# Moving 32x32 blocks by way of DRAM on one queue, an unrolled loop, and a later take-up of the moved blocks

## The chip, the cores and the metric

One core of one Trainium2 chip. The metric is the device time of one execution in microseconds; the kernel before has a median of 2729.89 us in 3 runs (2728.75 to 2730.19).

## The reference

Two transformer blocks in a row on 256 tokens of width 2048, all in float32. Each block normalises its input, makes projections, mixes tokens (block one with two kinds of softmax attention, block two with a chunked recurrence and a gated attention), adds the result, runs a feed-forward network, and ends with a gated embedding. The change touches the two feed-forward networks and what leads in and out of them:

```
ff = jnp.square(jax.nn.relu(u2 @ w_up)) @ w_down                     # block one, width 8192
a, g = jnp.split(u @ w_up, 2, axis=-1)                               # block two, width 5632
a = causal_dwconv(a, conv_w, conv_b)
x = x + (jax.nn.gelu(a, approximate=False) * g) @ w_down
```

## The kernel before, in words

**Products.** Each float32 weight is split on the chip into a high and a low part, and each activation too, so that a product is three passes of TensorE: high by high, high by low, low by high. A *unit* is 512 output columns for 256 tokens over 16 tiles of 128 rows: 16 x 2 x 3 = 96 matmuls (L2259 to L2261). A unit is cut into eight *halves* of two tiles, 12 matmuls each.

**Weights.** SyncE's queue loads them (L402) in pieces of 1 MB, two halves each, into a ring of four (`raw`). For each half ScalarE makes the high part (`hi`, L642) and VectorE the low part (`lo`, L1344), into a ring of four slots (`split`). Both engines run three halves ahead of TensorE (`LEAD`): in step m of a unit they prepare half m+3, when TensorE has given a slot back, and then do what `after(m)` asks for. In `after(m)` TensorE is therefore in half m.

**Why blocks are moved.** A unit comes out with tokens on the partitions. The next product wants features there. VectorE transposes 32x32 blocks in place within 32 partitions (L1742, L1744 for the feed-forward units, L1395 for rows of the residual), into `cross`; what is left is to carry each 32-partition group to its place. `move_blocks` (L377) does this with 16 DMAs of 32 KB from SBUF to SBUF: eight on SyncE's queue (between two weight loads, by `wide_and_move`) and eight on GpSimd's. Each queue first waits for `blocks_made`. There are 47 such moves: 3 in `branch`, 16 in `ffn1`, 3 in `out2`, 22 in `ffn2` and `ffn2b`, 3 in the last down product.

**Who takes a move up.** ScalarE or VectorE waits for both queues (`wait_for_move`, L385):
- `ffn1` (block one, four turns of 4 up and 4 down units): ScalarE and VectorE make the operand `X2` of the down product (`finish`, L936 and L1752) at m = 4 and m = 12 of the two-unit step that follows; the last of a turn, `finish(3)`, is taken up at m = 4 of the first down step, and half 6 of that unit is the first to read it.
- `ffn2` (block two, eleven pairs of up units a and g): for a, ScalarE copies the moved block at m = 12 (L1258), VectorE runs the convolution at m = 13 (L2116 to L2122) and ScalarE the gelu at m = 14; for g, VectorE multiplies at m = 3 of the next step (`gate_hidden`, L2104), and `finish` follows at m = 4.
- `out2` and the last down product: ScalarE takes the moved rows up (`gained_hi_moved`, L702) four halves after the unit's end.

**Loops.** TensorE, ScalarE and VectorE run turn 0 of `ffn1` written out, turns 1 and 2 as a loop of two (L1025, L1852, L2534), and turn 3 written out again. SyncE runs all four as a loop.

GpSimd has little else: rows of gains, and `ple_kept`, a DRAM scratch that it writes (L601) and later reads back (L620); `gate_rows` is another (L605 to L611).

Of the kernel before, what the change touches and what calls it, by code (L numbers as in the profile page):

```python
# [176 lines left out]
def two_blocks(nc, a, out):  # L177
# [141 lines left out]
    moved_by_sp, moved_by_pool = sem("moved_by_sp"), sem("moved_by_pool")  # L319
    second_by_sp, second_by_pool = sem("second_by_sp"), sem("second_by_pool")  # L320
# [22 lines left out]
    OUT2 = DOWN = plan([wide2, wide2])  # L343
    DOWN3 = [(m // 4 % 2, "wide", X2, 2 * (m % 4), 2, m % 4 == 0, False) for m in range(8)]
# [25 lines left out]

    MIX_MOVES, FFN1_MOVES, OUT2_MOVES, FFN2_MOVES, DOWN3_MOVES = 0, 3, 19, 22, 44
    MIX_MOVED = [E[:, 4 * c:4 * c + 4, :].rearrange("p k t -> p (k t)") for c in range(3)]
    DOWN3_ROUTES = [(cross_flat, t_flat), (a_moved, g_moved), (cross_flat, t_flat)]
    DOWN3_BY_SP = [moved_by_sp, second_by_sp, moved_by_sp]
    DOWN3_BY_POOL = [moved_by_pool, second_by_pool, moved_by_pool]

    def move_blocks(queue, n, dst, quadrants, moved, src=cross_flat):  # L377

        queue.wait_ge(blocks_made, n + 1)
        for a in quadrants:  # L380
            for b in range(4):
                rows = src[32 * a:32 * a + 32].rearrange("p (q b c) -> p q b c", q=2, b=4)[:, :, b, :]
                queue.dma_start(dst[32 * b:32 * b + 32].rearrange("p (q a c) -> p q a c", q=2, a=4)[:, :, a, :], rows).then_inc(moved, 16)  # L383

    def wait_for_move(eng, n):  # L385

        eng.wait_ge(moved_by_sp, 128 * (n + 1))
        eng.wait_ge(moved_by_pool, 128 * (n + 1))
# [5 lines left out]
    def _(sp):  # L394
# [54 lines left out]
        for n in range(4):  # L449
            s = at_triple("branch", n, 3 * n)  # L450
            wide(s, 0, w_in, 8192 + n * WIDE)
            wide(s, 4, a["w_br_moba"][0], n * WIDE, rows=512)
            if n:
                move_blocks(sp, MIX_MOVES + n - 1, MIX_MOVED[n - 1], (0, 1), moved_by_sp)
            wide(s, 5, a["w_br_moba"][0], n * WIDE, 512, 512)
            wide(s, 6, a["w_br_diff"][0], n * WIDE, rows=1024)
# [15 lines left out]
        def wide_and_move(at, w, col0, row0, n, dst):  # L472

            wide(at, 0, w, col0, row0, 512)
            if n is not None:
                move_blocks(sp, n, dst, (0, 1), moved_by_sp)
            wide(at, 1, w, col0, row0 + 512, 1536)

        def ffn1(b):
            for u in range(8):  # L480
                s = At("ffn1", g=4 * u, u=u, outer_turn=b * 8, outer_units=b * 8)
                n = FFN1_MOVES + b * 4 + (u - 2) if 2 <= u < 6 else None
                if u < 4:
                    wide_and_move(s, a["w_up"][0], b * 2048 + u * WIDE, 0, n, t_flat)
                else:
                    wide_and_move(s, a["w_down"][0], (u - 4) * WIDE, b * 2048, n, t_flat)
# [22 lines left out]
        for u in range(4):  # L509
            wide_and_move(At("out2", g=4 * u, u=u), a["w_out_2"][0], u * WIDE, 0, OUT2_MOVES + u - 2 if u > 1 else None, t_flat)  # L510

        def ffn2(name, b, pairs, c0):

            outer = dict(outer_turn=b * 12, outer_units=b * 12)
            col0 = c0 * WIDE

            def dst(u):
                return g_moved if u % 2 else a_moved

            for u in range(2 * pairs):  # L520
                n = FFN2_MOVES + 2 * c0 + u - 2 if u > 1 else OUT2_MOVES + 2 if c0 + u == 0 else None
                wide_and_move(At(name, g=4 * u, u=u, **outer), a["w_up_2"][0], u % 2 * FF2 + col0 + u // 2 * WIDE, 0, n, t_flat if c0 + u == 0 else dst(u))
            last = FFN2_MOVES + 2 * c0 + 2 * pairs - 2
            w = a["w_down_2"][0]
            if name == "ffn2":
                for n in range(4):
                    wide_and_move(At(name, g=8 * pairs + 4 * n, u=2 * pairs + n, **outer), w, n * WIDE, col0, last + n if n < 2 else None, dst(n))
            else:
                s = At(name, g=8 * pairs, u=2 * pairs)
                wide(s, 0, w, 0, col0, 512)  # L530
                move_blocks(sp, last, dst(0), (0, 1), moved_by_sp)
# [3 lines left out]
                move_blocks(sp, last + 1, dst(1), (0, 1), moved_by_sp)  # L535
# [3 lines left out]
                for n in range(2):  # L539
                    src, moved_to = DOWN3_ROUTES[n]  # L540
                    move_blocks(sp, DOWN3_MOVES + n, moved_to, (0, 1), DOWN3_BY_SP[n], src)
                    wide(s, 10 + n, w, 3 * WIDE, col0 + 512 + 512 * n, 512)
# [5 lines left out]
        move_blocks(sp, DOWN3_MOVES + 2, t_flat, (0, 1), moved_by_sp)  # L548
# [15 lines left out]
    def _(pool):  # L564
# [13 lines left out]
        for n in range(3):  # L578
            move_blocks(pool, MIX_MOVES + n, MIX_MOVED[n], (2, 3), moved_by_pool)
# [11 lines left out]
        for n in range(16):  # L591
            move_blocks(pool, FFN1_MOVES + n, t_flat, (2, 3), moved_by_pool)
# [21 lines left out]
        for n in range(3):  # L614
            move_blocks(pool, OUT2_MOVES + n, t_flat, (2, 3), moved_by_pool)
        for n in range(FFT2 // 2):
            move_blocks(pool, FFN2_MOVES + n, g_moved if n % 2 else a_moved, (2, 3), moved_by_pool)
# [3 lines left out]
        for n in range(3):  # L621
            src, moved_to = DOWN3_ROUTES[n]
            move_blocks(pool, DOWN3_MOVES + n, moved_to, (2, 3), DOWN3_BY_POOL[n], src)


    @block.scalar
    def _(act):
# [310 lines left out]
        def ffn1(b):  # L938
# [86 lines left out]
        loop(act, steps, 3, 0, ffn1, start=1)  # L1025
# [207 lines left out]
        def ffn2(name, b, pairs, c0):  # L1233
# [6 lines left out]
            def up(i):  # L1240
# [3 lines left out]
                def after(m):  # L1244
# [7 lines left out]
                    if m == 4 and i:  # L1252
                        finish(i - 1)
# [12 lines left out]
            def down(i):  # L1266
                each_half(At(name, i, 8, 2, g=8 * pairs, u=2 * pairs, **outer), DOWN, lambda m: finish(pairs - 1) if i == 0 and m == 4 else None)

            def last_down(s):

                def after(m):
                    if m == 4:
                        finish(pairs - 1)
                    if m in (14, 16, 22):
# [3 lines left out]
                        if n == 1:  # L1278
                            act.wait_ge(second_by_sp, 128)
                            act.wait_ge(second_by_pool, 128)  # L1280
                        else:
                            wait_for_move(act, DOWN3_MOVES + n // 2)
# [49 lines left out]
    def _(dve):  # L1332
# [421 lines left out]
        def ffn1(b):  # L1754
# [7 lines left out]
            def up(i):  # L1762
                s = At("ffn1", i, 8, 2, **outer)

                def after(m):
# [6 lines left out]
                    if m == 4 and i:  # L1772
                        finish(2 * i - 1)
                    if m == 12:
# [77 lines left out]
        loop(dve, steps, 3, 0, ffn1, start=1)  # L1852
# [244 lines left out]
        def ffn2(name, b, pairs, c0):  # L2097
# [27 lines left out]
            def up(i):  # L2125
# [3 lines left out]
                def after(m):  # L2129
# [6 lines left out]
                    if m == 3 and i:  # L2136
                        gate_hidden(i - 1)
                    if m == 4 and i:
# [7 lines left out]
            def finish_last(m):  # L2146
                if m == 3:
                    gate_hidden(pairs - 1)
                if m == 4:
                    finish(pairs - 1)  # L2150

            def down(i):
                s = At(name, i, 8, 2, g=8 * pairs, u=2 * pairs, **outer)

                def after(m):
                    if i == 0:
                        finish_last(m)
                    if m % 8 == 7:
                        add_h(s, m, m // 8, 2 * i + m // 8)
                each_half(s, DOWN, after)  # L2160
# [66 lines left out]
    def _(pe):  # L2227
# [306 lines left out]
        loop(pe, Chain(None), 3, 0, ffn1, start=1)  # L2534
# [148 lines left out]
        def ffn2(name, b, pairs, c0):  # L2683
# [12 lines left out]
            if name == "ffn2":  # L2696
                for i in range(2):
                    each_half(At(name, i, 8, 2, g=8 * pairs, u=2 * pairs, **outer), DOWN, hidden)
# [36 lines left out]
```

## Time and profile before

| what | value |
|---|---|
| median of 3 runs | 2729.89 us |
| the profiled execution | 2728.78 us, its span 2726.8 us |
| TensorE busy | 2715.3 us of the span, at the full granted clock throughout |
| VectorE, ScalarE, GpSimd busy | 1640.6, 1395.3, 220.0 us |
| DMA engines busy | 5 to 6 tenths in most slices |
| moved by DMA | 546.93 MB |

How to read it: an engine's busy time counts its own instructions, not its waiting for semaphores; DMA issues count on GpSimd and not on SyncE. The time of an idle stretch stands in front of the instruction that ended it, with what released it; "issue" means that the profile shows nothing that the engine waited for.

### The profile page before, as it was taken

How to read it: one execution, taken by the hardware profiler on the slowest of the kernel's cores; microseconds unless marked ns; L12 is line 12 of the kernel's file. 1: busy time of each engine (PE TensorE's matmuls, PEld its weight loads, DVE VectorE, ACT ScalarE, POOL GpSimd, SP SyncE). 2: the span in 40 equal slices, each digit the busy share in tenths (PEclk: the TensorE clock that was granted, in tenths of full speed). 3: DMA queues.
4: the chain of work that ended last, by engine and by line, in shares of the span. 5: the costliest groups of instructions: out<-in, count | busy, mean ns of one | idle time of the engine just before them, and what ended most of it. 6: DMA issues, size and time to landing. Idle time of an engine off the chain costs nothing.

```text
span 2726.8 us, 33571 instructions
## 1 busy us (share of the span) xinstructions
PE 2715.3 (100%) x12786; PEld 2267.8 (83%) x12786; DVE 1640.6 (60%) x2002; ACT 1395.3 (51%) x1851; POOL 220.0 (8%) x410
## 2 busy tenths in 40 slices
PE   9999999999999999999999999999999999999999
PEld 7888888888888878888888888888888888888887
DVE  7666665556555555555566656665666566656665
ACT  6454554446544535445466555655545345435553
POOL 0000000100100101101000000001111011101210
PEclk9999999999999999999999999999999999999999
DMA  8555556665666656656656655556666566656674
GB/s 300 174 181 185 170 176 207 204 203 182 211 213 200 219 191 201 215 179 220 221 176 221 193 162 180 169 170 215 200 218 224 190 203 207 233 189 220 219 244 139
DMA packets 344770, 546.93 MB, mean 201 GB/s; under 512 B 20548, under 2 KB 135184, under 8 KB 343984
## 3 DMA queue, kind: packets, MB, share of 16 engines
q1 hardware_dynamic: 330016, 522.98, 57.9%
q0 software_dynamic: 14608, 21.93, 3.1%
q8 instruction: 100, 1.64, 0.2%
q14 instruction: 46, 0.38, 0.0%
HBM read 515.98 MB, written 4.21 MB: 191 GB/s over the span
## 4 chain that ended last, share of the span: by engine, by line
PE 96%; DVE 2%; ACT 1%; issue 0%; DMA 0%; POOL 0%; SPq 0%; ACTq 0%; DVEq 0%
PE ps L2259 26%; PE ps L2260 25%; PE ps L2261 25%; PE ps L2249 11%; PE ps L2251 6%; DVE split L1344 1%; PE pw L2397 0%; PE pw L2364 0%; PE pw L2322 0%; PE pw L2375 0%; PE pw L2370 0%; ACT split L642 0%; DMA G<-cross 0%; PE pw L2363 0%; PE pw L2613 0%
## 5 line engine op out<-in xcount | busy, mean ns | idle before, releaser
L1344 DVE TENSOR_TENSOR split<-raw,split 128x1024 fp32r<-128x1024 f32 x960 | 1167.3, 1222 | 901.6 <-ACT split L642 899.9
L642 ACT ACTIVATE split<-raw 128x1024 fp32r<-128x1024 f32 x960 | 1009.9, 1058 | 1018.6 <-PE ps L2261 903.4
L2259 PE MATMUL ps<-split,X 128*128 128x512 f32 x3128 | 1221.8, 391 | 2.0 <-DVE split L1344 1.1
L2260 PE MATMUL ps<-split,X 128*128 128x512 f32 x3128 | 1217.2, 389 | 1.7 <-issue 1.7
L2261 PE MATMUL ps<-split,X 128*128 128x512 f32 x3128 | 1217.4, 389 | 0.0
L2259 PEld LDWEIGHTS ps<-split,X 128*128 128x128 f32 x3128 | 587.1, 188 | 125.6 <-issue 3.0
L2260 PEld LDWEIGHTS ps<-split,X 128*128 128x128 f32 x3128 | 587.2, 188 | 122.8 <-issue 2.1
L2261 PEld LDWEIGHTS ps<-split,X 128*128 128x128 f32 x3128 | 587.1, 188 | 122.3
L2249 PE MATMUL ps<-X,split 128*128 128x512 f32 x896 | 282.8, 397 | 0.2 <-DVE split L1344 0.2
L2251 PEld LDWEIGHTS ps<-X,split 128*128 128x128 f32 x896 | 168.3, 188 | 39.7
L2251 PE MATMUL ps<-X,split 128*128 128x256 f32 x896 | 176.1, 278 | 0.0
L383 POOL DMA_DIRECT2D t<-cross x168 | 89.8, 542 | 962.2 <-DVE cross L1744 562.5
L2249 PE MATMUL ps<-split,X 128*128 128x512 f32 x512 | 162.8, 399 | 0.0
L383 POOL DMA_DIRECT2D G<-cross x176 | 93.9, 542 | 583.7 <-DVE cross L1744 561.3
L2249 PEld LDWEIGHTS ps<-X,split 128*128 128x128 f32 x896 | 137.0, 189 | 1.7 <-issue 1.0
L2251 PEld LDWEIGHTS ps<-split,X 128*128 128x128 f32 x512 | 96.2, 188 | 22.7
L2251 PE MATMUL ps<-split,X 128*128 128x256 f32 x512 | 100.7, 278 | 0.0
L2249 PEld LDWEIGHTS ps<-split,X 128*128 128x128 f32 x512 | 78.2, 189 | 0.6 <-issue 0.4
L927 ACT ACTIVATE t<-ps,norm_col 128x512 f32<-128x512 f32 x76 | 47.9, 681 | 43.0 <-PE ps L2261 43.0
L648 ACT ACTIVATE cross<-ps 128x512 f32<-128x512 f32 x44 | 26.3, 597 | 66.5 <-PE ps L2251 66.3
L1742 DVE STREAM_TRANSPOSE cross<-t 128x512 f32<-128x512 f32 x38 | 27.0, 709 | 48.7 <-ACT t L975 37.9
L1262 ACT ACTIVATE G<-G,cols 128x256 f32<-128x256 f32 x44 | 18.8, 498 | 32.1 <-DVE G L2122 32.1
(271 smaller groups left out, 1083.3 us busy)
## 6 DMA issues: line engine op xcount, KB each, us to landing
raw<-in_w_up SPq DMA_DIRECT2D x152, 1024.0 KB, 5.3
raw<-in_w_in SPq DMA_DIRECT2D x134, 1024.0 KB, 5.1
raw<-in_w_down SPq DMA_DIRECT2D x108, 1024.0 KB, 5.2
raw<-in_w_out SPq DMA_DIRECT2D x32, 1024.0 KB, 5.1
raw<-in_w_ple_gate SPq DMA_DIRECT2D x32, 1024.0 KB, 5.2
raw<-in_w_br_moba SPq DMA_DIRECT2D x8, 1024.0 KB, 5.2
raw<-in_w_br_diff SPq DMA_DIRECT2D x8, 1024.0 KB, 6.8
G<-cross SPq DMA_DIRECT2D x176, 32.0 KB, 1.9
```

What stands on the lines that cost most here:

```text
L383: queue.dma_start(dst[32 * b:32 * b + 32].rearrange("p (q a c) -> p q a c", q=2, a=4)[:, :, a, :], rows).then_inc(moved, 16)
L642: A(split[:, k % RING, :, 0, :], raw[:, (k // 2) % RING, HALF * (k % 2):HALF * (k % 2) + HALF, :], ACT.Copy).then_inc(hi_done, 1)
L648: A(cross[:, s], ps[:, 2 * s:2 * s + 2, TOK:512], ACT.Copy).then_inc(cross_done, 1)
L927: ins = A(t_tok[:, q, :], ps[:, bank + q, :], func, scale=norm_col[:, k, q:q + 1])
L1262: ins = A(gelu[:, j, :], conv[:, j, :], ACT.Gelu, bias=vec("conv_b_2", 4 * c + j))
L1344: TT(split[:, k % RING, :, 1, :], raw[:, (k // 2) % RING, HALF * (k % 2):HALF * (k % 2) + HALF, :], split[:, k % RING, :, 0, :], ALU.subtr ...
L1742: nc.vector.transpose(cross_tok[:, 0, :], by_blocks(t_tok[:, 0, :]))
L2249: MM(ps[:, 2 * s + j, :], stay[:, 0, j * P:j * P + P], move, start=start, stop=False, skip_group_check=True)
L2251: ins = MM(ps[:, 2 * s + j, 0:TOK], stay[:, 1, j * P:j * P + P], move[:, 0, :], start=False, stop=stop, skip_group_check=True)
L2259: MM(dst, x_hi, w[:, :, 0, :], start=start, stop=False, skip_group_check=True)
L2260: MM(dst, x_hi, w[:, :, 1, :], start=False, stop=False, skip_group_check=True)
L2261: ins = MM(dst, x_lo, w[:, :, 0, :], start=False, stop=stop, skip_group_check=True)
```

## The change: what it does

- A move is four writes of 128 KB from `cross` to a DRAM scratch (two scratches in turn, `blocks_kept`), a wait on GpSimd until all four have landed, and one read of 512 KB back to the destination. All five are on GpSimd's queue; SyncE's queue carries no moves any more.
- The three loops over turns 1 and 2 of `ffn1` are written out.
- Take-up is later: in `ffn1` m = 4 and 12 of the up steps become 5 and 13; in `ffn2` m = 3 and 4 become 5 and 6. ScalarE's copy of a at m = 12, `finish(3)` at m = 4 of the first down step of `ffn1`, and the take-up in `out2` and in the last down product at m = 14, 16, 22 stay.
- The first two down units of each `ffn2` are interleaved (`DOWN2`): 12 tiles of unit 0, 12 tiles of unit 1, then the last 4 of each, and SyncE loads the weights in that order. The last 4 tiles are those of the last pair.

```diff
-    def move_blocks(queue, n, dst, quadrants, moved, src=cross_flat):
-
-        queue.wait_ge(blocks_made, n + 1)
-        for a in quadrants:
-            for b in range(4):
-                rows = src[32 * a:32 * a + 32].rearrange("p (q b c) -> p q b c", q=2, b=4)[:, :, b, :]
-                queue.dma_start(dst[32 * b:32 * b + 32].rearrange("p (q a c) -> p q a c", q=2, a=4)[:, :, a, :], rows).then_inc(moved, 16)
+    def move_blocks(pool, n, dst, src=cross_flat):
+
+        pool.wait_ge(blocks_made, n + 1)
+        kept = blocks_kept[n % 2]
+        for a in range(4):
+            rows = src[32 * a:32 * a + 32].rearrange("p (q b c) -> p q b c", q=2, b=4)
+            pool.dma_start(kept.rearrange("(b i) (q a c) -> i q b a c", b=4, q=2, a=4)[:, :, :, a, :], rows).then_inc(blocks_left[n % 2], 16)
+        pool.wait_ge(blocks_left[n % 2], 64 * (n // 2 + 1))
+        pool.dma_start(dst, kept).then_inc(blocks_back[n % 2], 16)
 
     def wait_for_move(eng, n):
 
-        eng.wait_ge(moved_by_sp, 128 * (n + 1))
-        eng.wait_ge(moved_by_pool, 128 * (n + 1))
+        eng.wait_ge(blocks_back[n % 2], 16 * (n // 2 + 1))
...
+    DOWN2 = [(m // 6, "wide", X2, 2 * (m % 6), 2, m % 6 == 0, False) for m in range(12)]
+    DOWN2 += [(m // 2, "wide", X2, 12 + 2 * (m % 2), 2, False, m % 2 == 1) for m in range(4)]
...
-                    wide_and_move(s, a["w_up"][0], b * 2048 + u * WIDE, 0, n, t_flat)
+                    wide(s, 0, a["w_up"][0], b * 2048 + u * WIDE)
...
-                    if m == 4 and i:
+                    if m == 5 and i:
                         finish(2 * i - 1)
-                    if m == 12:
+                    if m == 13:
                         finish(2 * i)
...
-                    if m == 3 and i:
+                    if m == 5 and i:
                         gate_hidden(i - 1)
-                    if m == 4 and i:
+                    if m == 6 and i:
                         finish(i - 1)
...
-                each_half(s, DOWN, after)
+                    if m in ((7, 15) if i else (13, 15)):
+                        add_h(s, m, m // 15, 2 * i + m // 15)
+                each_half(s, DOWN if i else DOWN2, after)
...
-        loop(pe, Chain(None), 3, 0, ffn1, start=1)
+        ffn1(1)
+        ffn1(2)
         ffn1(3)
```

The same three lines stand for ScalarE and VectorE.

## Rows read from the trace of the kernel before

**Rows 1.** The page: the span, and busy us, share and instructions by engine.

```profile
span 2726.8 us, 33571 instructions
PE 2715.3 (100%) x12786; PEld 2267.8 (83%) x12786; DVE 1640.6 (60%) x2002; ACT 1395.3 (51%) x1851; POOL 220.0 (8%) x410
```

**Rows 2.** Stretches of 68 us: busy us and instructions by engine, clock, DMA.

```profile
884.00:952.00 68.00, 68.00 (x301) 56.31 (x301) 37.89 (x37) 36.26 (x44) 12.80 (x24) 1.00 0.66 218
...
1020.00:1088.00 68.00, 66.29 (x292) 54.54 (x291) 34.57 (x33) 32.20 (x38) 8.53 (x16) 1.00 0.62 203
...
2312.00:2380.00 68.00, 67.31 (x297) 55.45 (x297) 42.56 (x49) 33.00 (x38) 12.81 (x24) 1.00 0.67 224
...
2652.00:2720.00 68.00, 68.00 (x302) 56.31 (x301) 37.05 (x38) 29.38 (x31) 0.00 (x0) 1.00 0.45 152
```

**Rows 3.** Timeline of TensorE, 1017 to 1025 us: start, duration, what.

```profile
1019.24 0.49 PE L2259 MATMUL ps<-split,X 128*128 128x512 f32 x1 [0.16 <-issue]
...
1022.83 0.50 PE L2260 MATMUL ps<-split,X 128*128 128x512 f32 x1 [1.71 <-issue]
```

**Rows 4.** Timelines around 2310 to 2327 us, by engine, in order of time.

```profile
2310.21 0.67 DVE L1744 STREAM_TRANSPOSE cross<-t 128x512 f32<-128x512 f32 x1
...
2314.27 4.28 POOL L383 DMA_DIRECT2D G<-cross  x8 [22.17 <-issue]
...
2316.03 10.94 SPq L402 DMA_DIRECT2D raw<-in_w_up  x3
...
2324.21 1.23 DVE L2104 TENSOR_TENSOR G<-G 128x1024 f32<-128x1024 f32 x1 [6.65 <-DMA G<-cross]
...
2326.71 0.47 PE L2259 MATMUL ps<-split,X 128*128 128x512 f32 x1 [0.69 <-DVE split L1344]
```

**Rows 5.** GpSimd's DMA issues by line: count, busy us, mean ns of one.

```profile
L601 POOL DMA_DIRECT2D ple_kept<-E x4 | 2.9, 721 | 41.6 <-ACT E L906 41.6
L583 POOL DMA_DIRECT2D sg<-in_w_in x3 | 3.5, 1166 | 37.9 <-DVE G L1670 37.9
```

**Rows 6.** Timeline of GpSimd, 1511 to 1530 us: a write to DRAM, its read.

```profile
1512.86 0.53 POOL L607 DMA_DIRECT2D gate_rows<-E  x1 [3.96 <-DVE E L1933]
1515.40 0.57 POOL L609 DMA_DIRECT2D G<-gate_rows  x1 [2.01 <-DMA gate_rows<-E]
```

**Rows 7.** DMA issues: KB each, median us from issue to landing.

```profile
G<-cross POOLq DMA_DIRECT2D x176, 32.0 KB, 1.8
...
ple_kept<-E POOLq DMA_DIRECT2D x4, 512.0 KB, 4.3
...
E<-ple_kept POOLq DMA_DIRECT2D x2, 1024.0 KB, 10.3
...
G<-gate_rows POOLq DMA_DIRECT2D x1, 512.0 KB, 5.8
```

**Rows 8.** Timelines of VectorE and ScalarE, 758 to 784 us (`ffn1`, `finish(3)`).

```profile
760.65 0.67 DVE L1744 STREAM_TRANSPOSE cross<-t 128x512 f32<-128x512 f32 x1
...
768.94 1.06 ACT L642 ACTIVATE split<-raw 128x1024 fp32r<-128x1024 f32 x1 [1.66 <-PE ps L2261]
769.90 1.14 ACT L936 ACTIVATE X<-t 128x512 fp32r<-128x512 f32 x2
...
771.17 1.29 DVE L1752 TENSOR_TENSOR X<-t,X 128x512 fp32r<-128x512 f32 x2
```

**Rows 9.** Timelines of three engines, 2240 to 2284 us (`ffn2`, a unit a).

```profile
2243.10 0.67 DVE L1744 STREAM_TRANSPOSE cross<-t 128x512 f32<-128x512 f32 x1
...
2244.06 4.26 POOL L383 DMA_DIRECT2D G<-cross  x8 [15.67 <-DVE cross L1744]
...
2253.65 1.04 ACT L1258 ACTIVATE E<-G 128x1024 f32<-128x1024 f32 x1
2255.40 1.06 ACT L642 ACTIVATE split<-raw 128x1024 fp32r<-128x1024 f32 x1 [0.71 <-PE ps L2261]
...
2262.10 1.22 DVE L1344 TENSOR_TENSOR split<-raw,split 128x1024 fp32r<-128x1024 f32 x1
```

More of the change, by code:

```diff
@@ L318, in two_blocks @@
     tokens_kept, blocks_made, padded = (sem(n) for n in ("tokens_kept", "blocks_made", "padded"))
-    moved_by_sp, moved_by_pool = sem("moved_by_sp"), sem("moved_by_pool")
-    second_by_sp, second_by_pool = sem("second_by_sp"), sem("second_by_pool")
+    blocks_left, blocks_back = ([sem(f"{name}{k}") for k in range(2)] for name in ("blocks_left", "blocks_back"))
     out_landed = sem("out_landed")
@@ L369, in squared @@
         return 8 * (k - 1)
+    blocks_kept = [nc.dram_tensor(f"blocks_kept{k}", (P, 1024), F32).ap() for k in range(2)]
     MIX_MOVES, FFN1_MOVES, OUT2_MOVES, FFN2_MOVES, DOWN3_MOVES = 0, 3, 19, 22, 44
@@ L451, in _ @@
             wide(s, 0, w_in, 8192 + n * WIDE)
[L452 to L455, printed above, removed]
+            wide(s, 4, a["w_br_moba"][0], n * WIDE, rows=1024)
             wide(s, 6, a["w_br_diff"][0], n * WIDE, rows=1024)
@@ L470, in _ @@
         proj("proj1", a["w_ple_proj"][0])
[L472 to L477, printed above, removed]
         def ffn1(b):
@@ L481, in ffn1 @@
                 s = At("ffn1", g=4 * u, u=u, outer_turn=b * 8, outer_units=b * 8)
-                n = FFN1_MOVES + b * 4 + (u - 2) if 2 <= u < 6 else None
                 if u < 4:
-                    wide_and_move(s, a["w_up"][0], b * 2048 + u * WIDE, 0, n, t_flat)
+                    wide(s, 0, a["w_up"][0], b * 2048 + u * WIDE)
                 else:
-                    wide_and_move(s, a["w_down"][0], (u - 4) * WIDE, b * 2048, n, t_flat)
+                    wide(s, 0, a["w_down"][0], (u - 4) * WIDE, b * 2048)
         loop(sp, Chain(None), 4, 0, ffn1)
@@ L509, in _ @@
         for u in range(4):
-            wide_and_move(At("out2", g=4 * u, u=u), a["w_out_2"][0], u * WIDE, 0, OUT2_MOVES + u - 2 if u > 1 else None, t_flat)
+            wide(At("out2", g=4 * u, u=u), 0, a["w_out_2"][0], u * WIDE)
         def ffn2(name, b, pairs, c0):
@@ L515, in ffn2 @@
             col0 = c0 * WIDE
-            def dst(u):
-                return g_moved if u % 2 else a_moved
             for u in range(2 * pairs):
-                n = FFN2_MOVES + 2 * c0 + u - 2 if u > 1 else OUT2_MOVES + 2 if c0 + u == 0 else None
-                wide_and_move(At(name, g=4 * u, u=u, **outer), a["w_up_2"][0], u % 2 * FF2 + col0 + u // 2 * WIDE, 0, n, t_flat if c0 + u == 0 else dst(u))
-            last = FFN2_MOVES + 2 * c0 + 2 * pairs - 2
+                wide(At(name, g=4 * u, u=u, **outer), 0, a["w_up_2"][0], u % 2 * FF2 + col0 + u // 2 * WIDE)
             w = a["w_down_2"][0]
             if name == "ffn2":
-                for n in range(4):
-                    wide_and_move(At(name, g=8 * pairs + 4 * n, u=2 * pairs + n, **outer), w, n * WIDE, col0, last + n if n < 2 else None, dst(n))
+                s = At(name, g=8 * pairs, u=2 * pairs, **outer)
+                wide(s, 0, w, 0, col0, 512)
+                wide(s, 1, w, 0, col0 + 512, 1024)
+                wide(s, 3, w, WIDE, col0, 1024)
+                wide(s, 5, w, WIDE, col0 + 1024, 512)
+                wide(s, 6, w, 0, col0 + 1536, 512)
+                wide(s, 7, w, WIDE, col0 + 1536, 512)
+                for n in range(2, 4):
+                    wide(s, 4 * n, w, n * WIDE, col0)
             else:
@@ L530, in ffn2 @@
                 wide(s, 0, w, 0, col0, 512)
-                move_blocks(sp, last, dst(0), (0, 1), moved_by_sp)
                 wide(s, 1, w, 0, col0 + 512, 512)
@@ L534, in ffn2 @@
                 wide(s, 4, w, 0, col0 + 1024, 512)
-                move_blocks(sp, last + 1, dst(1), (0, 1), moved_by_sp)
                 wide(s, 5, w, WIDE, col0 + 1024, 512)
@@ L538, in ffn2 @@
                 wide(s, 9, w, 3 * WIDE, col0, 512)
[L539 to L542, printed above, removed]
+                wide(s, 10, w, 3 * WIDE, col0 + 512, 1024)
         ffn2("ffn2", 0, 4, 0)
@@ L547, in _ @@
         wide(At("gate2"), 0, w, 0, 0, 1024)
-        move_blocks(sp, DOWN3_MOVES + 2, t_flat, (0, 1), moved_by_sp)
         wide(At("gate2"), 2, w, 0, 1024, 1024)
@@ L578, in _ @@
         for n in range(3):
-            move_blocks(pool, MIX_MOVES + n, MIX_MOVED[n], (2, 3), moved_by_pool)
+            move_blocks(pool, MIX_MOVES + n, MIX_MOVED[n])
         pool.wait_ge(gated, 4)
@@ L591, in _ @@
         for n in range(16):
-            move_blocks(pool, FFN1_MOVES + n, t_flat, (2, 3), moved_by_pool)
+            move_blocks(pool, FFN1_MOVES + n, t_flat)
         pool.wait_ge(hid_ready, 32)
@@ L614, in _ @@
         for n in range(3):
-            move_blocks(pool, OUT2_MOVES + n, t_flat, (2, 3), moved_by_pool)
+            move_blocks(pool, OUT2_MOVES + n, t_flat)
         for n in range(FFT2 // 2):
-            move_blocks(pool, FFN2_MOVES + n, g_moved if n % 2 else a_moved, (2, 3), moved_by_pool)
+            move_blocks(pool, FFN2_MOVES + n, g_moved if n % 2 else a_moved)
         pool.wait_ge(hid_ready, 32 + FFT2 // 2)
@@ L622, in _ @@
             src, moved_to = DOWN3_ROUTES[n]
-            move_blocks(pool, DOWN3_MOVES + n, moved_to, (2, 3), DOWN3_BY_POOL[n], src)
+            move_blocks(pool, DOWN3_MOVES + n, moved_to, src)
     @block.scalar
@@ L1024, in _ @@
         A(gate_split[:, :, 16:32], gate_w[:, :, :], ACT.Copy, scale=0.0).then_inc(gate_split_hi, 1)
-        loop(act, steps, 3, 0, ffn1, start=1)
+        ffn1(1)
+        ffn1(2)
         ffn1(3)
@@ L1266, in down @@
             def down(i):
-                each_half(At(name, i, 8, 2, g=8 * pairs, u=2 * pairs, **outer), DOWN, lambda m: finish(pairs - 1) if i == 0 and m == 4 else None)
+                each_half(At(name, i, 8, 2, g=8 * pairs, u=2 * pairs, **outer), DOWN if i else DOWN2, lambda m: finish(pairs - 1) if i == 0 and m == 6 else None)
             def last_down(s):
                 def after(m):
-                    if m == 4:
+                    if m == 6:
                         finish(pairs - 1)
@@ L1277, in after @@
                         square_h(8, n)
[L1278 to L1282, printed above, removed]
+                        wait_for_move(act, DOWN3_MOVES + n)
                         gained_hi_moved(n, "ple_norm_g_2", DOWN3_ROUTES[n][1])
@@ L1771, in after @@
                             norm_inverse(2)
-                    if m == 4 and i:
+                    if m == 5 and i:
                         finish(2 * i - 1)
-                    if m == 12:
+                    if m == 13:
                         finish(2 * i)
@@ L1851, in _ @@
         TT(gate_split[:, :, GATE_LO:GATE_LO + 16], gate_w[:, :, :], gate_split[:, :, 0:16], ALU.subtract).then_inc(gate_split_lo, 1)
-        loop(dve, steps, 3, 0, ffn1, start=1)
+        ffn1(1)
+        ffn1(2)
         ffn1(3)
@@ L2135, in after @@
                             norm_inverse(7)
-                    if m == 3 and i:
+                    if m == 5 and i:
                         gate_hidden(i - 1)
-                    if m == 4 and i:
+                    if m == 6 and i:
                         finish(i - 1)
@@ L2146, in finish_last @@
             def finish_last(m):
-                if m == 3:
+                if m == 5:
                     gate_hidden(pairs - 1)
-                if m == 4:
+                if m == 6:
                     finish(pairs - 1)
@@ L2157, in after @@
                         finish_last(m)
-                    if m % 8 == 7:
-                        add_h(s, m, m // 8, 2 * i + m // 8)
-                each_half(s, DOWN, after)
+                    if m in ((7, 15) if i else (13, 15)):
+                        add_h(s, m, m // 15, 2 * i + m // 15)
+                each_half(s, DOWN if i else DOWN2, after)
             def last_down(s):
@@ L2533, in _ @@
         ffn1(0)
-        loop(pe, Chain(None), 3, 0, ffn1, start=1)
+        ffn1(1)
+        ffn1(2)
         ffn1(3)
@@ L2697, in ffn2 @@
                 for i in range(2):
-                    each_half(At(name, i, 8, 2, g=8 * pairs, u=2 * pairs, **outer), DOWN, hidden)
+                    each_half(At(name, i, 8, 2, g=8 * pairs, u=2 * pairs, **outer), DOWN if i else DOWN2, hidden)
             else:
```

2 lines of the change are left out of this document (removed).

## The prediction

> **What bounds the kernel now.** I read the page first: TensorE is busy for 2715.3 of 2726.8 us [rows 1], so time can be won only where TensorE stands still, or lost where something new makes it stand still. Next the stretches of 68 us. A stretch of the feed-forward networks that holds 24 of GpSimd's move DMAs has 301 matmuls, and one at the end with none has 302 [rows 2]: a matmul every 68/301 = 0.226 us, a half of 12 matmuls every 2.71 us, with moves or without. In the stretches that the change touches, two fall clearly short: 292 from 1020 us and 297 from 2312 us [rows 2]. That is 9 + 4 = 13 missing matmuls, 13 x 0.226 = 2.9 us. What stood there is in the timelines. At 1019 and 1022 us TensorE is idle for 0.16 and 1.71 us and waits for nothing the profile knows [rows 3]; this is where the loop over turns 1 and 2 of `ffn1` jumps back. At 2326 us it waits 0.69 us for a low part [rows 4]: VectorE stood 6.65 us before L2104, because one move, ready when the transposes ended at 2310.88, came late: GpSimd began its DMAs only at 2314.27 (3.4 us late, the cause not in the profile), and its last ones ran into three weight loads issued from 2316.03 [rows 4]. So at most 2.9 us, 0.11%, can be won here.
>
> **What each part costs or gives.**
>
> Loops written out: the same matmuls in the same order, without a jump. Gives the idle at 1019 and 1022 us, 9 x 0.226 = 2.0 us. ScalarE's and VectorE's loops cost nothing before, since both run ahead of TensorE.
>
> Later take-up: the late move at 2310.88 landed 2324.2 - 2310.88 = 13.3 us after its transposes and cost 4 x 0.226 = 0.9 us [rows 2, 4], so L2104 at m = 3 bears a landing up to 13.3 - 0.9 = 12.4 us; at m = 5 it bears two halves more, 12.4 + 5.4 = 17.8 us. That returns the 0.9 us if a hiccup like it comes again. The last pair would then be finished at m = 6 of a down unit whose half 6 reads it; `DOWN2` reads it from step 12 instead, 6 x 2.71 = 16 us after the take-up, so this costs nothing. Interleaving keeps every matmul; the third unit starts at step 16, and the first one's sums are read from step 13, 5.4 us earlier in TensorE's time than they are needed. If VectorE were late there by more, TensorE would wait at step 16.
>
> SyncE's queue: 47 x 8 DMAs and 47 waits leave it. Nothing waits for it (no weight load shows among TensorE's releasers in [rows 3, 4]), so this gives nothing by itself. But the eight DMAs held weight loads back during a move; now loads run beside every move, as at 2316 us.
>
> GpSimd's queue: 16 short DMAs on two queues become four writes, a wait and a read on one. Behind the new wait stand the next move, the gain rows and the read-back of `ple_kept`; moves come one per unit, 96 x 0.226 = 21.7 us apart, except in the last down product, where the second follows two halves after the first and would start behind its read. Three moves there and three in `out2` keep their take-up four halves after the unit's end; each is a single event of a us or so and is left to the range. For the time from the transposes' end to landing, no row shows the very thing, so step by step:
> - start: 2244.06 - 2243.77 = 0.3 us [rows 9];
> - three issues before the last write: 0.54 each for 64 pieces (4.26/8) [rows 9], 1.17 for 2048 pieces [rows 5]; I take 0.72, `ple_kept` with as many pieces as here, 256 [rows 5]: 2.2 us;
> - last write issued to read issued: the small write to `gate_rows` took 1515.40 - 1512.86 = 2.5 us [rows 6]; the 512 KB write to `ple_kept` 4.3 to land [rows 7], plus 0.3 to start again, 4.6. At 128 KB I take the middle, 3.5;
> - the read, 512 KB: between 1.8 (32 KB from SBUF) and 10.3 (1 MB of `ple_kept`); I take 5.8, the read of 512 KB of `gate_rows`, the same size on the same queue [rows 7].
>
> Sum 0.3 + 2.2 + 3.5 + 5.8 = 11.8 us; ends 0.3 + 1.6 + 2.5 + 1.8 = 6.2 and 0.3 + 3.5 + 4.6 + 10.3 = 18.7. The Trainium skill ("DMA: Bandwidth & Descriptors", Anatomy of one DMA) gives 2.0 us and bytes/436e3 per DMA from GpSimd and warns that most of the 2 us is the write receipt, longest for HBM. By its figures the estimate would be about 0.3 + 2.2 + 2.6 + 3.2 = 8.3 us, but it would put 3.2 us on a 512 KB write and the row has 4.3, so the rows decide.
>
> What bears 11.8 us? Two take-ups were not made later.
> - `finish(3)`, four times: transposes end at 761.32, half 4 starts about 768.9, so half 6, the first reader, at 768.9 + 5.4 = 774.3. Before it lie one L936 (half of 1.14) and one L1752 (half of 1.29), together 1.2 us [rows 8]. The limit is 774.3 - 1.2 - 761.3 = 11.8 us.
> - ScalarE's copy of a, eleven times: transposes end at 2243.77, the copy starts at 2253.65, 9.9 us later. A later start first uses up 0.71 us of ScalarE's idle before L642 at 2255.40. Then it pushes the convolution and the low part behind it, which ends at 2263.3; the slot that L642 fills at 2255.4 is read three halves later, the next one at 2255.4 + 4 x 2.71 = 2266.2, so 2.9 us are left [rows 9]. The limit is 9.9 + 0.7 + 2.9 = 13.5 us.
>
> At 11.8 us the first limit is just met and the second holds with 1.7 us in hand: cost 0. Each us past 11.8 costs 4 us in all, past 13.5 another 11, past 17.8 (g) another 11.
>
> **Sum.** Against the profiled execution, 2728.78 (span 2726.8 and 2.0 around it): 2728.78 - 2.0 - 0.9 = 2725.9. It lies 1.1 below the median of 2729.89, so 2727.0 on the scale of the medians. About 0.2% (5.5 us) is what a measurement of this kernel can tell from no change; this is half of it.
>
> **Rivals.**
> 1. *The round trip outlasts the slack* (0.13). Place: L936 in `finish(3)` and L1258. For it: loads now run beside every move, and beside loads 32 KB DMAs had the late move end at 13.3 us. Against it: the rows used for 5.8 and 4.3 ran beside weight loads too, and the slack is measured. At 15 us it costs 4 x 3.2 + 11 x 1.5 = 29 us: 2756. It turns the sign past the 0.2% at 2727.0 + 4d = 2735.4, d = 2.1, a landing of about 13.7 us (the eleven add 2 there); at the upper end, 18.7 us, it is 4 x 6.9 + 11 x 5.2 + 11 x 0.9 = 95 us, 2822.
> 2. *The change does not do what it seems to* (0.13). The idle at 1022 us is "issue", so that the jump causes it is my reading; written-out code could stall likewise at another place, and a slow start of GpSimd like that at 2310.88 can fall on a move of a, where 11.8 + 3.1 = 14.9 us passes both limits once. Then 2730.
> 3. *TensorE's pace itself rises* (0.04), because transfers no longer go from SBUF to SBUF. One ns per matmul is 12786 ns: 2714. Against it stand 301 matmuls with moves and 302 without [rows 2].
>
> **How the numbers follow.** My case, landing under 13.3 us and the jump's idle gone, has 0.70: 2727.0, from 2725.0 (the lowest run, 2728.75, less 2.9, and 0.8 for chance) to 2727.0 + 4 x 1.5 = 2733. Rivals 1, 2 and 3 have 0.13, 0.13 and 0.04. The range 2725 to 2733 holds my case and rival 2, 0.83; the two others, 0.17, are left out, and so are the extreme ends of the landing. Faster by over 0.2% is rival 3, slower is rival 1, the rest is the same.
>
> **What would show it.** Right: no idle of TensorE over 1 us after 700 us; 301 matmuls in every stretch inside a feed-forward network; the last of `cross`'s four writes landing about 5.7 us after the transposes and the read 11.8; ScalarE's L1258 waiting for a DMA by up to 2 us and TensorE for nothing. Wrong: TensorE waiting for a low part once per pair of up units at regular distance, or for L1752 at half 6 of each turn's first down unit; an "issue" gap inside turns 1 or 2 of `ffn1`; a read that lands within 8 us, which would make the step-by-step cost too high though not the time; a changed pace in a stretch without gaps.

## The result and the profile after

The changed kernel takes 2805.91 us (median of 6 runs, 2802.20 to 2811.39) against 2729.92 us before: a ratio of 1.0281 [1.0271, 1.0291], slower by 76 us. The forecast was 2727.0, a small gain, with a range of 2725 to 2733; the change came out as a loss, far outside the range. What happened is rival 1, the round trip outlasting the slack, at a higher price than the rival had been given. The profiled execution took 2802.2 us, with a span of 2800.4.

The page of the changed kernel, its span and engines, the chain that ended last, and DMA issues with the median from issue to landing:

```profile
span 2800.4 us, 32690 instructions
...
PE 2738.1 (98%) x12786; PEld 2275.8 (81%) x12786; DVE 1635.5 (58%) x2002; ACT 1390.0 (50%) x1851; POOL 160.2 (6%) x269
...
PE 78%; DMA 10%; DVE 7%; ACT 2%; issue 2%; POOL 2%; ACTq 0%; POOLq 0%; DVEq 0%
...
blocks_kept<-cross POOLq DMA_DIRECT2D x184, 128.0 KB, 5.8
G<-blocks_kept POOLq DMA_DIRECT2D x23, 512.0 KB, 6.2
t<-blocks_kept POOLq DMA_DIRECT2D x21, 512.0 KB, 4.5
```

Beside [rows 1], TensorE stands still for 2800.4 - 2738.1 = 62.3 us instead of 11.5, and needs 22.8 us more for the same 12786 matmuls. DMA now has 10% of the chain that ended last. A write of 128 KB takes 5.8 us, and the estimate for the whole way from the last write's issue to the read's issue had been 3.5.

The loss by stage, from the stretches of the changed kernel (columns as in [rows 2]; the first one answers to the stretch with the jump, the next four are `ffn1`, `out2`, `ffn2` with its down units, and the last down product):

```profile
1020.00:1088.00 68.00, 68.00 (x301) 56.31 (x301) 36.70 (x34) 32.93 (x39) 5.99 (x10) 1.00 0.67 217
...
700.00:1420.00 720.00, 715.07 (x3164) 590.41 (x3163) 392.76 (x380) 345.01 (x414) 48.25 (x81) 1.00 0.66 216
...
1885.00:1935.00 50.00, 43.22 (x186) 34.84 (x185) 23.66 (x31) 23.92 (x41) 3.55 (x6) 0.97 0.55 188
...
1935.00:2670.00 735.00, 702.92 (x3031) 573.37 (x3030) 417.35 (x478) 328.39 (x380) 70.92 (x119) 0.98 0.64 216
...
2670.00:2715.00 45.00, 34.64 (x140) 27.82 (x139) 22.37 (x28) 20.96 (x36) 5.13 (x9) 0.89 0.55 184
```

The stretch from 1020 us has its 301 matmuls, where [rows 2] had 292: the jump's idle is gone. For the others, the length less 68/301 = 0.226 us per matmul is what the stretch lost: 720 - 3164 x 0.2259 = 5.2 us in `ffn1`, 8.0 in `out2`, 50.3 in `ffn2`, 13.4 in the last product. Their sum, 76.9, is the whole loss: it equals the difference to the span of the kernel `late_sbuf` below (2723.4), which has everything of the change but the new way of moving (77.0). Of the 50.3 in `ffn2`, 735 - 702.92 = 32.1 are idle; the rest is TensorE running slower, at a mean granted clock of 0.98.

The waits of the changed kernel (us in total, times, longest):

```profile
POOL G L385 <- DMA blocks_kept<-cross: 130.3, 22, 7.0
POOL t L385 <- DMA blocks_kept<-cross: 121.6, 21, 7.1
...
ACT E L1245 <- DMA G<-blocks_kept: 76.9, 11, 9.8
DVE G L2088 <- DMA G<-blocks_kept: 54.6, 11, 6.0
...
ACT X L922 <- DVE G L2088: 52.3, 11, 5.8
...
PE ps L2243 <- DVE split L1327: 43.1, 24, 3.7
...
PE pw L2306 <- DVE h L2060: 6.7, 2, 6.3
PE ps L2243 <- DVE X L1735: 4.4, 4, 1.5
```

TensorE waits 24 times for a low part (43.1 us) and four times for `finish(3)` (4.4), the signs that were named for "wrong", though not once per pair: 17 of the 24 stand in `ffn2` with its eleven pairs. ScalarE's copy of a (L1245, before L1258) waits 7.0 us on average, VectorE's `gate_hidden` (L2088, before L2104) 5.0, although its take-up is two halves later than in [rows 4].

One pair in `ffn2` of the changed kernel, by engine, in order of time: first the move of g, then the move of a.

```profile
1972.79 11.49 SPq L403 DMA_DIRECT2D raw<-in_w_up  x4
...
1976.13 0.67 DVE L1727 STREAM_TRANSPOSE cross<-t 128x512 f32<-128x512 f32 x1
...
1977.09 2.44 POOL L383 DMA_DIRECT2D blocks_kept<-cross  x4 [16.50 <-DVE cross L1727]
1986.16 0.56 POOL L385 DMA_DIRECT2D G<-blocks_kept  x1 [6.64 <-DMA blocks_kept<-cross]
1992.37 1.23 DVE L2088 TENSOR_TENSOR G<-G 128x1024 f32<-128x1024 f32 x1 [5.77 <-DMA G<-blocks_kept]
1993.63 1.16 ACT L922 ACTIVATE X<-G 128x512 fp32r<-128x512 f32 x2 [5.57 <-DVE G L2088]
1995.64 1.24 ACT L913 ACTIVATE t<-ps,norm_col 128x512 f32<-128x512 f32 x2
...
1997.61 0.67 DVE L1727 STREAM_TRANSPOSE cross<-t 128x512 f32<-128x512 f32 x1
...
1998.57 2.44 POOL L383 DMA_DIRECT2D blocks_kept<-cross  x4 [11.85 <-DVE cross L1727]
1999.42 6.64 SPq L403 DMA_DIRECT2D raw<-in_w_up  x3
2003.34 1.06 ACT L628 ACTIVATE split<-raw 128x1024 fp32r<-128x1024 f32 x1 [1.66 <-PE ps L2245]
2007.91 0.56 POOL L385 DMA_DIRECT2D G<-blocks_kept  x1 [6.90 <-DMA blocks_kept<-cross]
2014.16 1.06 ACT L1245 ACTIVATE E<-G 128x1024 f32<-128x1024 f32 x1 [9.76 <-DMA G<-blocks_kept]
2016.19 1.22 DVE L1327 TENSOR_TENSOR split<-raw,split 128x1024 fp32r<-128x1024 f32 x1 [10.54 <-ACT split L628]
2017.34 1.14 DVE L2100 TENSOR_SCALAR G<-E,cols 128x256 f32<-128x256 f32 x4
...
2021.81 1.22 DVE L1327 TENSOR_TENSOR split<-raw,split 128x1024 fp32r<-128x1024 f32 x1
2017.56 0.47 PE L2243 MATMUL ps<-split,X 128*128 128x512 f32 x1 [3.44 <-DVE split L1327]
2019.06 0.63 PE L2243 MATMUL ps<-split,X 128*128 128x512 f32 x1
...
2021.19 0.63 PE L2245 MATMUL ps<-split,X 128*128 128x512 f32 x1
2023.17 0.47 PE L2243 MATMUL ps<-split,X 128*128 128x512 f32 x1 [1.35 <-DVE split L1327]
```

Three readings. **The move is long because loads run beside it.** SyncE issues 1 MB weight loads beside both moves, four from 1972.79 and three from 1999.42; the four writes of a, issued from 1998.57, let GpSimd read back only at 2007.91, and ScalarE's copy starts at 2014.16, 2014.16 - 1998.28 = 15.9 us after the transposes' end. **One late move costs more than one wait.** The copy's delay uses up the lead, so TensorE waits 3.44 us at 2017.56. Then VectorE's convolution (from 2017.34; its three steps take 1.14, 1.67 and 1.67 us) stands between two low parts with no lead left: the next one starts only at 2021.81, and TensorE waits again, 1.35 us at 2023.17. **In between TensorE is slow.** From 2019.06 to 2021.19 a matmul comes every 0.426 us instead of 0.226 (five intervals in 2.13 us). The granted clock of that stretch is 0.50, that is 1.2 GHz, the lower of the clock's two levels; shortly before, the engine had stood still for 3.44 us.

### The profile page after: what moved, and what is told of

The parts are those of the page before. It is cut to its first block, busy times and chain, and to the rows that moved or that the text cites. A ratio compares the mean times of both kernels' runs of the same rounds, so it can differ in the third digit from the quotient of the medians.

```text
span 2800.4 us, 32690 instructions
## 1 busy us (share of the span) xinstructions
PE 2738.1 (98%) x12786; PEld 2275.8 (81%) x12786; DVE 1635.5 (58%) x2002; ACT 1390.0 (50%) x1851; POOL 160.2 (6%) x269
## 4 chain that ended last, share of the span: by engine, by line
PE 78%; DMA 10%; DVE 7%; ACT 2%; issue 2%; POOL 2%; ACTq 0%; POOLq 0%; DVEq 0%
PE ps L2243 19%; PE ps L2245 19%; PE ps L2244 19%; PE ps L2233 11%; PE ps L2235 6%; DMA blocks_kept<-cross 5%; DMA G<-blocks_kept 3%; DVE split L1327 2%; POOL blocks_kept L383 2%; DMA t<-blocks_kept 1%; ACT split L628 1%; DVE G L2103 1%; DVE G L2106 1%; DVE cross L1725 0%; DVE cross L1727 0%
## 5 line engine op out<-in xcount | busy, mean ns | idle before, releaser
L2243 PE MATMUL ps<-split,X 128*128 128x512 f32 x3128 | 1230.9, 394 | 48.1 <-DVE split L1327 43.1
L383 POOL DMA_DIRECT2D blocks_kept<-cross x184 | 112.3, 617 | 1507.5 <-DVE cross L1727 1025.5
L913 ACT ACTIVATE t<-ps,norm_col 128x512 f32<-128x512 f32 x76 | 47.7, 679 | 30.8 <-PE ps L2245 28.0
L1245 ACT ACTIVATE E<-G 128x1024 f32<-128x1024 f32 x11 | 11.7, 1061 | 76.9 <-DMA G<-blocks_kept 76.9
L2088 DVE TENSOR_TENSOR G<-G 128x1024 f32<-128x1024 f32 x11 | 13.5, 1226 | 54.6 <-DMA G<-blocks_kept 54.6
```

The lines of the kernel that those rows point to most:

```text
L383: pool.dma_start(kept.rearrange("(b i) (q a c) -> i q b a c", b=4, q=2, a=4)[:, :, :, a, :], rows).then_inc(blocks_left[n % 2], 16)
L913: ins = A(t_tok[:, q, :], ps[:, bank + q, :], func, scale=norm_col[:, k, q:q + 1])
L2243: MM(dst, x_hi, w[:, :, 0, :], start=start, stop=False, skip_group_check=True)
```

## Experiments

The theory after the result: the new way of moving alone is to blame, because the eight DMAs of SyncE's queue that it removes had kept weight loads away while blocks moved. In the kernel before, SyncE's queue shows this in one pair (timelines of SyncE and, for later, of ScalarE):

```profile
2243.80 5.08 SPq L383 DMA_DIRECT2D G<-cross  x8
2248.92 6.47 SPq L402 DMA_DIRECT2D raw<-in_w_up  x3
...
2252.68 1.06 ACT L642 ACTIVATE split<-raw 128x1024 fp32r<-128x1024 f32 x1 [1.66 <-PE ps L2261]
```

The next load was issued only after the eight transfers, 5.1 us after the move began. Rivals: the written-out loops or the new order of take-up and down units cost the time; or a round trip through DRAM is too slow in itself, loads or not.

**late_sbuf**: the changed kernel's loops, take-up and down order, but the 16 transfers between SBUF partitions on two queues as before. Against the changed kernel, among others:

```diff
+        queue.wait_ge(blocks_made, n + 1)
+        for a in quadrants:
+            for b in range(4):
+                rows = src[32 * a:32 * a + 32].rearrange("p (q b c) -> p q b c", q=2, b=4)[:, :, b, :]
+                queue.dma_start(dst[32 * b:32 * b + 32].rearrange("p (q a c) -> p q a c", q=2, a=4)[:, :, a, :], rows).then_inc(moved, 16)
```

> The written-out loops, the later take-up and DOWN2 of the change, but each move still 16 transfers from SBUF to SBUF on two queues. Theory A (the whole loss comes from the moves through DRAM): 2727 us, 2 to 3 us under the kernel before, no idle of TensorE over 1 us after 700 us. Rival B (interleaving the down units or taking blocks up later costs time by itself): between 2735 and 2805 us, with TensorE waiting in the first down step of each ffn2 or two halves after a unit's end.

Measured: 2725.25 us (11 runs) against 2729.52 for the kernel before (28 runs), ratio 0.9984 [0.9975, 0.9993], span 2723.4. So the whole loss comes from the new way of moving, and the rest of the change gains a little. This run puts back two things at once, the transfers within SBUF and the eight DMAs on SyncE's queue; the runs below tell them apart.

**unrolled**: the kernel before with nothing but the three loops written out.

```diff
-        loop(pe, Chain(None), 3, 0, ffn1, start=1)
+        ffn1(1)
+        ffn1(2)
         ffn1(3)
```

> The kernel before with only the three loops over turns 1 and 2 of ffn1 written out. If the jump makes the idle at 1019 and 1022 us: 2.0 us less than before, 2728 us, and no issue gap inside ffn1. If written-out code stalls elsewhere: 2730 us with an issue gap at another place.

Measured: 2725.99 us (11 runs), ratio 0.9988 [0.9979, 0.9997]: 3.5 us less where 2.0 were expected, by the interval 0.8 to 5.7. Its stretch from 1020 us:

```profile
1020.00:1088.00 68.00, 68.00 (x302) 56.31 (x301) 35.99 (x35) 34.88 (x41) 8.96 (x17) 1.00 0.61 202
```

302 matmuls instead of 292: the jump had caused the "issue" idle. TensorE waits for "issue" nowhere in this run, and the first half of rival 2 falls.

**hold_writes** and **hold_move**: the changed kernel, but SyncE waits at the places where it used to issue its eight DMAs (after the first load of a unit): in one until the four writes have landed, in the other until the read has. No DMA is added. SyncE's loop over the turns of `ffn1` is written out for it.

```diff
+    def hold_loads(sp, n):
+        sp.wait_ge(blocks_left[n % 2], 64 * (n // 2 + 1))     # hold_writes
+        sp.wait_ge(blocks_back[n % 2], 16 * (n // 2 + 1))     # hold_move
```

> The changed kernel, with SyncE's queue waiting, at the places where it issued moves before, until the four writes of the move have landed; only then does it issue further weight loads (and SyncE's loop over ffn1 is written out). Theory C (the writes take 6 us because a weight load is issued beside the third one): the writes land by about 5 us after the transposes instead of 8.2, the read about 11.5 instead of 13.9, time 2730 to 2745 us. Rival I (four writes of 512-byte pieces to DRAM on GpSimd's queue take 8 us whatever runs beside them): writes 8.2, read 12 to 14, time 2790 us or more.

> As hold_writes, but SyncE waits until the read of the move has landed too. Theory C: read back 9 us after the transposes, below every limit, time about 2727 us. Rival I: the move still takes 12 us or more, time over 2780 us; should the held loads themselves come too late, TensorE would wait for ScalarE's high parts released by a DMA of raw.

Measured: hold_writes 2739.27 us (5 runs), ratio 1.0038 [1.0025, 1.0051]; hold_move 2725.40 us (10 runs), ratio 0.9984 [0.9975, 0.9994]. The DMA issues of hold_writes:

```profile
blocks_kept<-cross POOLq DMA_DIRECT2D x184, 128.0 KB, 2.7
G<-blocks_kept POOLq DMA_DIRECT2D x23, 512.0 KB, 6.6
```

and of hold_move:

```profile
blocks_kept<-cross POOLq DMA_DIRECT2D x184, 128.0 KB, 2.7
G<-blocks_kept POOLq DMA_DIRECT2D x23, 512.0 KB, 3.5
```

The same write takes 2.7 us with the loads held and 5.8 beside them (the changed kernel), the same read 3.5 and 6.6 (hold_writes, which lets the loads go when the read starts). In hold_move a whole move reads like this (timelines of GpSimd, SyncE and ScalarE):

```profile
1980.55 2.43 POOL L383 DMA_DIRECT2D blocks_kept<-cross  x4 [14.39 <-DVE cross L1752]
1985.41 0.56 POOL L385 DMA_DIRECT2D G<-blocks_kept  x1 [2.44 <-DMA blocks_kept<-cross]
1988.90 2.98 SPq L407 DMA_DIRECT2D raw<-in_w_up  x3
...
1990.13 1.04 ACT L1270 ACTIVATE E<-G 128x1024 f32<-128x1024 f32 x1
```

The transposes ended at 1980.25 and the loads, released by the landing, start again at 1988.90: 8.65 us for the move. ScalarE's copy comes in its turn and waits for nothing. Holding the loads gives back all 80 us between the changed kernel and this one, with every byte still going through DRAM; so the round trip is not too slow in itself, the loads beside it are the cause. Holding during the writes alone already returns 67 us; the read beside loads keeps 13.9.

**a_later**: the changed kernel with ScalarE's copy of a at m = 14, the convolution at m = 0 of the next step and the gelu at m = 2.

```diff
-                    if m == 12:
+                    if m == 14:
...
-                    if m == 13:
-                        convolve(c)
+                    if m == 0 and i:
+                        convolve(c - 1)
```

> The changed kernel with only the chain of a taken up later: ScalarE copies the moved a at m = 14 instead of 12, VectorE convolves at m = 0 of the next step instead of m = 13, ScalarE's gelu follows at m = 2. Theory L (the loss in ffn2 is ScalarE waiting in order for a block that lands 13 to 17 us after its transposes, and the convolution that then stands between two low parts): that take-up is 15.3 us after the transposes, so TensorE's waits in the eleven pairs go; left are about 5 us in finish(3), 7 in out2, 9 in the last down product and some at the lower clock: 2745 to 2765 us. Rival Q (the loss follows the lateness of g, or GpSimd's queue as a whole, not the place where a is taken up): over 2785 us.

Measured: 2750.74 us, ratio 1.0082 [1.0065, 1.0099], in the range expected. The waits of a_later:

```profile
PE ps L2253 <- DVE split L1335: 8.8, 6, 3.5
...
DVE G L2096 <- DMA G<-blocks_kept: 8.1, 10, 2.1
...
PE ps L2253 <- DVE X L1743: 3.4, 4, 1.1
```

The moves are about as slow as in the changed kernel (the writes have a median of 5.5 us instead of 5.8), and yet 55 us are gone, somewhat more than the 50.3 that `ffn2` had lost. What `gate_hidden` waits for g fell from 54.6 to 8.1 us though nothing about g was changed. So the late a had made g wait; that a late g delays the next a is worked out below, under the copy of a. What is left is 2750.74 - 2725.25 = 25.5 us. None of it is in the pairs: from 1935 to 2620 us TensorE is busy throughout at a granted clock of 1.00. By the measure used above, `ffn1` with its four `finish(3)` loses 4.1 us, `out2` 7.1 and the last product 10.9.

**early**: the changed kernel with the take-up and the down order of the kernel before.

```diff
-                    if m == 5 and i:
+                    if m == 3 and i:
                         gate_hidden(i - 1)
...
-                each_half(s, DOWN if i else DOWN2, after)
+                each_half(s, DOWN, after)
```

> The changed kernel with the take-up and the order of the down units of the kernel before (m = 4 and 12 in ffn1, m = 3 and 4 in ffn2, no DOWN2). Theory L: L2104 bears a landing 12.4 us after the transposes and g lands at 12.6 to 15.7, so every pair waits twice: 2830 to 2870 us. Rival (the later take-up gained nothing because a is what waits): 2806 us, as the changed kernel.

Measured: 2816.62 us (2 runs), ratio 1.0321 [1.0301, 1.0342]. A miss: slower by 11 us where at least 24 were expected. The waits of early:

```profile
DVE G L2082 <- DMA G<-blocks_kept: 93.3, 11, 9.2
...
ACT E L1239 <- DMA G<-blocks_kept: 47.4, 11, 6.7
...
PE ps L2237 <- DVE X L1729: 14.1, 6, 5.6
```

The wait for g grows from 54.6 to 93.3 us, but the one for a falls from 76.9 to 47.4. The sum of the two hardly changes (131.5 and 140.7), and TensorE's waits for low parts grow only from 43.1 to 44.7 us. So with moves this late the later take-up is worth little inside the pairs. The 11 us are elsewhere: of the 14.1 us that TensorE waits for `finish` (L1729), two waits of 5.6 us stand in the first down step of the two `ffn2`, where the changed kernel, with `DOWN2` there, has none.

**hold_early**: hold_move with the take-up and the down order of the kernel before.

> hold_move (weight loads held until the read of a move has landed, 8.6 us after the transposes) with the take-up and down order of the kernel before. Theory L: 8.6 us is under the limits of 11.8, 12.4 and 13.5 us, so 2725 to 2728 us, though L2104, due 6.6 us after the transposes, waits some 2 us for a DMA each time. Rival (a move through DRAM needs the later take-up): over 2735 us.

Measured: 2725.15 us (10 runs), ratio 0.9986 [0.9976, 0.9995]; `gate_hidden` waits 23.7 us in all at m = 3, and TensorE does not lose by it. With the loads held, the later take-up is not needed.

**pool_sbuf**: late_sbuf with all 16 SBUF transfers on GpSimd's queue and none on SyncE's. It takes the DRAM out and leaves the loads unheld.

```diff
+        if quadrants == (0, 1):
+            return
-        for a in quadrants:
+        for a in range(4):
```

> late_sbuf with all 16 SBUF transfers of a move on GpSimd's queue and none on SyncE's, so that weight loads run beside the moves as in the changed kernel, but nothing goes through DRAM. Alone, 0.3 + 16 x 0.54 + 1.3 = 10.2 us from the transposes to the last landing. Theory C1 (any small transfer beside a weight load lands late; what the change lost is the hold on the loads): transfers that land 1.8 us after their issue when alone take 4 to 6 us when a load is issued beside them, the move lands at 12 to 14 us, time 2735 to 2770 us. Rival C2 (only transfers to or from DRAM suffer): the move lands by 10.5 us, under the limits of 11.8 and 13.5 us, time 2725 to 2728 us.

Measured: 2771.77 us (4 runs), ratio 1.0157 [1.0140, 1.0174], just over the expected range. The DMA issues of pool_sbuf:

```profile
G<-cross POOLq DMA_DIRECT2D x352, 32.0 KB, 4.9
t<-cross POOLq DMA_DIRECT2D x336, 32.0 KB, 4.6
```

The same 32 KB take 1.8 us in [rows 7] and in late_sbuf. That 16 of them stand on one queue is not the reason: of the move issued from 1947.65, the first two landed after 1.7 us, and those issued from 1949.25 on, after a load at 1948.83, after 3.3 to 4.9 us. So it is not only DRAM transfers that suffer beside the loads; these short ones within SBUF do too, and what the change lost is the hold on the loads. Without any DRAM that costs 2771.77 - 2725.25 = 46.5 us; with the longer way through DRAM it costs 80.

Four of these kernels beat both the one before and the changed one: hold_early, late_sbuf, hold_move and unrolled, 2725.15 to 2725.99 us. Their gains are 0.12 to 0.16%, with intervals below 1 that overlap, so the four are not told apart.

## Why the prediction was wrong, point by point

- **What bounds the kernel, and what can be won**: right within the noise. 2.9 us were said to be there at most; `unrolled` and `late_sbuf` have spans 3.0 and 3.4 us shorter than the one before (2726.8), and medians 3.5 and 4.3 us lower, with intervals that reach below 2.9. The loops' term, 2.0 us by the profile, lies inside the measured 0.8 to 5.7.
- **Later take-up and `DOWN2` at no cost**: right; in late_sbuf TensorE waits for no low part longer than 0.3 us and for no `finish`. With the moves as late as in the changed kernel, the run without `DOWN2` (early) lost 11 us there.
- **"SyncE's queue ... this gives nothing by itself."** This is the step that failed. The next sentence of the prediction named what happens ("the eight DMAs held weight loads back during a move; now loads run beside every move") and put no price on it. It was worth 80 us, the difference of hold_move and the changed kernel: partly by the longer round trip, partly by the limits that shrank under it, as the next points tell.
- **The round trip, term by term.** Start: 0.3 predicted, 1977.09 - 1976.80 = 0.3. Three issues: 2.2 predicted, 3 x 0.61 = 1.8 (2.44 for four). Last write issued to read issued: 3.5 predicted, 130.3/22 + 0.6 = 6.5 by the waits of L385. Read: 5.8 predicted, 6.2 into `G` and 4.5 into `t`. The sums are 14.8 and 13.0 us instead of 11.8; the third term alone is 3 us too low, while the others are off by less and mostly to the other side. The rows it was taken from were a lone small write (2.5) and a 512 KB write (4.3) [rows 6, 7]; between 2.7 and 5.8 it is the load beside the write that decides.
- **"The rows used for 5.8 and 4.3 ran beside weight loads too"**: this was the argument against rival 1. For the read it holds: it was issued at 1515.40 and a load at 1515.45, and its 5.8 compares with 4.5 to 6.2. The write's 4.3 is a median over different cases. Of the four 512 KB writes to `ple_kept` in the kernel before, the one issued at 1473.38, with no load issued between 1465.82 and 1476.08, landed after 3.1 us; the one at 1477.00, right behind the load at 1476.08, after 5.9. And no load was issued within the lone small write of 2.5. So the trace of the kernel before already had the price of a load beside a write, hidden in the median.
- **The rule against the rows.** By the Trainium skill ("DMA: Bandwidth & Descriptors", Anatomy of one DMA) the estimate for the move was 8.3 us. The rows decided for 11.8. With the loads held hold_move has 8.65 us, near the first; with loads beside it the changed kernel has 13.0 to 14.8, above both. The Trainium skill gives that figure per DMA, and that section of it says nothing of a load beside one. Another section of the same page of the Trainium skill (Issuing engines are not separate DMA queues) says that transfers interleave on the same 16 DMA engines whichever engine issued them. The changed kernel, hold_writes, hold_move and pool_sbuf agree with that, 2.7 against 5.8, 3.5 against 6.6 and 1.8 against 4.9 us.
- **`finish(3)`, limit 11.8**: right. Its move at 760.85 (transposes' end) was taken up at 773.44, 12.6 us later; four such cost TensorE 4.4 us by the waits, and 4 x 0.8 = 3.2 was the formula.
- **The copy of a, limit 13.5**: right only where nothing was late ahead of it. In the kernel before step 12 begins at 2252.68 (the L642 just before the copy of [rows 9], shown above), 8.9 us after the transposes' end. In the changed kernel it begins 8.8 to 8.9 us after in three moves of eleven, the first a of each group of pairs; in the other eight it begins 5.0 to 7.5 us after, in the one shown at 2003.34, 5.1 us after. Of these 3.8 us, 3.1 went because `finish` on ScalarE (L922, at m = 6) waited 5.57 us for the late g, and the eviction of the next unit (L913) stood behind it: step 8 began at 2003.34 - 4 x 2.71 = 1992.5, the eviction at 1995.64. The limit shrinks with it, to 13.5 - 3.8 = 9.7 us: a landing at 15.9 is then 6.2 too late, and 3.44 + 1.35 of waiting and 1.0 of slow matmuls, 5.8 us, were lost there. So the formula's 11 x (14.8 - 13.5) = 14 us became 50.3: two moves, each within its own limit or nearly, push one another. The limit of 17.8 for g had looked only at TensorE's readers, and not at what stands behind L922 on ScalarE.
- **`out2` and the last product**, "left to the range": 8.0 and 13.4 us, together more than the whole range.
- **The clock** was in no term: part of the 22.8 us that TensorE is busier are matmuls at the lower level after a wait.
- **Rivals 2 and 3** are not what cost the time: the jump was the cause of the idle (`unrolled`), nothing stalls in the written-out code instead, and TensorE's pace did not rise where nothing waits, 301 matmuls in the stretch from 1020 us. A stop of GpSimd did fall on a move of a once, but a short one: 1.35 us of "issue" before the write at 2280.30.
- **Rival 1's price**: 2756 at 15 us, too low by 50 for the limits that shrank, the two stages left out and the clock; its chance of 0.13 was too small for a part whose main condition, loads beside every move, was certain by the code. (By its own formula the sign turns at a landing of 13.6 us, not 13.7: 4 x 1.8 + 11 x 0.1 = 8.3.)

What stays open: how the DMA engines share their time so that a 32 KB transfer lands some 3 us later beside loads. That in the changed kernel a read into `t` lands faster (4.5) than one into `G` (6.2) is not due to the destination: with the loads held both take 3.5 (hold_move), with loads let go at the read's start 6.8 and 6.6 (hold_writes).

## What to carry to other kernels

A transfer that is removed from a queue may have been holding back what follows it there. Before it goes, ask what the queue will issue in its place, and what that will run beside: here a bulk load beside a short transfer made it take about two to nearly three times as long. If short transfers are on the path, let the queue of bulk loads wait for them; in hold_move that cost TensorE nothing, though ScalarE waited for a load five times, 7.3 us in all (once, 1.4 us, in the kernel before). And a limit for one late arrival holds only while nothing else on the same engine is late: look at what is queued behind the waiting instruction, up to the eviction that starts the next arrival.

## What was not expected of the hardware

- What runs beside a transfer mattered as much as its size or where it goes: 1.8 to 4.9 us for 32 KB within SBUF, 2.7 to 5.8 for 128 KB to DRAM, 3.5 to 6.6 for 512 KB from it, with 1 MB weight loads issued beside it in each second number.
- A wait of TensorE is not paid when it ends. After 3.44 us of standing still six matmuls came at 0.23 to 0.31 us each, and then they came every 0.426 us at a granted clock of 0.50, though nothing was waited for: five such intervals cost another 5 x 0.2 = 1.0 us. In the last down product, the stretch with the longest wait (6.3 us), the mean granted clock was 0.89.
